# The order of sums over rows, gate products and slot matrices in a mixture-of-experts stage

## What is computed

```python
def expert_block(args):
    xb, gb = args
    h = jax.nn.silu(jnp.einsum('td,edf->tef', xb, w_gate)) * jnp.einsum('td,edf->tef', xb, w_up)
    h = h * gb[..., None].astype(h.dtype)
    return jnp.einsum('tef,efd->td', h, w_down)
```

## Time and profile before

| | us |
|---|---|
| median of 3 runs | 1060.3 |
| lowest and highest | 1058.49, 1063.44 |
| the profiled execution | 1058.91 |
| its span, first to last instruction | 1056.7 |
| PE busy | 959.5 (91%) |
| VectorE busy | 530.8 (50%) |

### The profile page before, as it was taken

The page is one execution under the profiler, slowest core; times in us unless marked ns, Lnnn a source line. Parts: engine busy times, 40 slices in busy tenths (PEclk is TensorE's granted clock), DMA queues, the critical chain, the costliest instruction groups (busy, mean ns, idle before and its releaser), DMA issues.

```text
span 1056.7 us, 18183 instructions
## 1 busy us (share of the span) xinstructions
PE 959.5 (91%) x7418; PEld 567.7 (54%) x7418; DVE 530.8 (50%) x1061; ACT 234.4 (22%) x486; POOL 328.4 (31%) x362
## 2 busy tenths in 40 slices
PE   5999999999999987699998989979999999998995
PEld 4878877877787776448433334333333343333331
DVE  2148957875986678766133222121323223346665
ACT  3241134114312511433111111111111111111013
POOL 0049906961993499000111111010100110024310
PEclk9999999999999999899998889998999999999998
DMA  8635244525434247198799999999999999999951
GB/s 231 177 120 191 101 135 140 191 82 159 154 112 141 73 165 274 25 382 335 268 390 418 420 413 406 419 409 401 386 419 410 404 411 411 421 414 415 363 220 42
DMA packets 87358, 291.98 MB, mean 276 GB/s; under 512 B 17084, under 2 KB 48382, under 8 KB 62423
## 3 DMA queue, kind: packets, MB, share of 16 engines
q1 hardware_dynamic: 72647, 254.03, 62.7%
q0 software_dynamic: 14624, 36.74, 9.2%
HBM read 275.48 MB, written 32.63 MB: 292 GB/s over the span
## 4 chain that ended last, share of the span: by engine, by line
PE 66%; DMA 18%; DVE 8%; issue 3%; ACT 2%; SPq 2%; POOL 0%; DVEq 0%; POOLq 0%
PE bank L1358 63%; DMA big<-in_w_up 16%; PE bank L595 2%; ACT big L1655 2%; DMA big<-yrows,big 1%; DMA big<-in_w_in 1%; DVE big L1945 1%; SPq L400 1%; PE bank L626 1%; DVE big L1056 1%; DVE big L1998 1%; DVE big L990 1%; DVE big L2002 0%; ACT L1655 0%; DVE big L1153 0%
## 5 line engine op out<-in xcount | busy, mean ns | idle before, releaser
L1358 PE MATMUL bank<-big 64*64 64x64 f32 (+8 forms) x6930 | 894.8, 357 | 75.9 <-DMA big<-in_w_up 23.5
L1358 PEld LDWEIGHTS bank<-big 64*64 64x64 f32 (+5 forms) x6930 | 511.5, 148 | 411.1 <-issue 317.2
L1655 ACT ACTIVATE big<-bank 128x512 f32<-128x512 f32 (+7 forms) x286 | 123.4, 453 | 659.6 <-PE bank L1358 385.5
L1159 POOL DMA_INDIRECT big<-xg,big x32 | 32.9, 1029 | 413.5 <-PE bank L595 337.3
L2149 POOL TENSOR_SCALAR big<-big 128x256 f32<-128x256 f32 x120 | 132.2, 1102 | 1.7
L981 DVE TENSOR_TENSOR big<-big,bank 128x256 f32<-128x256 f32 x32 | 13.5, 421 | 193.3 <-ACT big L1655 193.3
L2161 POOL TENSOR_TENSOR big<-big 128x256 f32<-128x256 f32 x120 | 94.3, 786 | 0.3
L1945 DVE SCALAR_TENSOR_TENSOR big<-big 128x256 f32<-128x256 f32 x120 | 79.6, 663 | 4.1
L990 DVE COPY big<-bank 128x512 f32<-128x512 f32 x32 | 22.1, 690 | 89.9 <-PE bank L1358 89.9
L1655 ACT ACTIVATE big<-big 128x272 f32<-128x272 f32 (+9 forms) x108 | 49.8, 505 | 42.3 <-DVE big L1880 11.3
L1655 ACT ACTIVATE big<-bank,big 128x272 f32<-128x272 f32 (+2 forms) x53 | 23.8, 476 | 112.4 <-PE bank L1358 112.4
(11 more groups left out here) (164 smaller groups left out, 443.5 us busy)
## 6 DMA issues: line engine op xcount, KB each, us to landing
big<-in_w_gate SPq DMA_DIRECT2D x64, 1024.0 KB, 15.2
big<-in_w_up SPq DMA_DIRECT2D x64, 1024.0 KB, 20.1
big<-in_w_down SPq DMA_DIRECT2D x64, 1024.0 KB, 12.7
big<-in_w_in SPq DMA_DIRECT2D x29, 1024.0 KB, 5.4
yrows<-big POOLq DMA_DIRECT2D x32, 512.0 KB, 3.5
big<-in_w_out SPq DMA_DIRECT2D x2, 2048.0 KB, 15.9
big<-in_state_wkv SPq DMA_DIRECT2D x32, 64.0 KB, 2.3
out_wkv_s<-big SPq DMA_DIRECT2D x32, 64.0 KB, 4.0
```

The lines of the kernel that those rows point to most:

```text
L1159: pool.indirect_dma_start(out=x[0:n, :], out_offset=None, in_=xg, in_offset=bass.IndirectOffsetOnAxis(ap=idxu[0:n, col:col + 1], axis=0), ...
L1358: return nc.tensor.matmul(out_, lhsT=lhsT, rhs=rhs, start=start, stop=stop)
L1655: return nc.scalar.activation(out_, in_, f, **kw)
```

## The change

On PE, `combine(q - 2)` stands behind the gate half `gate_up(q, 0, 4)` instead of ahead of it, and in those iterations `index(q + 3)` goes with it, behind the sum. In the other iterations the order is the old one. `turn_gates` waits for the first of the five additions of pair q-2 (the one that reads bank 0, which it writes) instead of for all five. On VectorE `late_gates` is split: the gate matrix (`gate_hots`) stands at the head of the iteration, then the slot matrix, then the additions; the copy of the turned gate matrix (`gate_copy`) stays behind the row list.

```diff
--- before.py
+++ after.py
@@ -653,7 +653,7 @@
 
                 pe.wait_ge(S['og_ready'], nlate(q) + 1)
                 wait(pe, 'g_ready', nlate(q))
-                wait(pe, 'cb_sum', NC * nlate(q - 1))
+                wait(pe, 'cb_sum', NC * nlate(q - 2) + (1 if late(q - 2) else 0))
                 pe.wait_ge(S['idx_ready'], 2 * min(q + 4, NPAIR))
                 for t in range(3):
                     r = tile_rows(t)
@@ -683,9 +683,7 @@
                     note(ins, 'cb_mm')
 
             for q in range(NPAIR):
-                if late(q - 2):
-                    combine(q - 2)
-                if q + 3 < NPAIR:
+                if q + 3 < NPAIR and not late(q - 2):
                     index(q + 3)
                 if q == 4:
                     count = pe.value_load(cnti[0:1, 0:1])
@@ -694,6 +692,10 @@
                 if DOWN_AT <= q < DOWN_AT + NDOWN:
                     shared_down(q - DOWN_AT)
                 gate_up(q, 0, 4)
+                if late(q - 2):
+                    combine(q - 2)
+                    if q + 3 < NPAIR:
+                        index(q + 3)
                 if q:
                     turn_hidden(q - 1)
                 if late(q):
@@ -990,14 +992,18 @@
                 note(v.tensor_copy(ye[q % NYE][:, 512:1024], ps_y[1][:, :]), 'ye_dve')
 
             def pair(q):
+                if late(q):
+                    gate_hots(q)
+                if q + 4 < NPAIR and late(q - 2):
+                    onehot(q + 4)
                 if late(q - 2):
                     add_late(q - 2)
                 if q + 3 < NPAIR:
                     fetch_rows(q + 3)
-                if q + 4 < NPAIR:
+                if q + 4 < NPAIR and not late(q - 2):
                     onehot(q + 4)
                 if late(q):
-                    late_gates(q)
+                    gate_copy(q)
                 ks = list(range(sums_by(q), sums_by(q + 1)))
                 ahead = len(ks) if q == NPAIR - 1 else len(ks) // 2
                 add_early(q, ks[:ahead])
@@ -1012,7 +1018,7 @@
                 if q == DOWN_AT + NDOWN - 1:
                     shared_rows(NDOWN - 1)
 
-            def late_gates(q):
+            def gate_hots(q):
                 wait(dve, 'g_mm', nlate(q))
                 link(v.tensor_tensor(OHg, K['slot'][:, 0:SLOTS].unsqueeze(1).unsqueeze(1)
                                      .broadcast_to([128, 3, 2, SLOTS]),
@@ -1020,6 +1026,8 @@
                                      ALU.is_equal), chain)
                 note(v.tensor_tensor(OHg, OHg, gate[:, :, 2 * PAIR[q]:2 * PAIR[q] + 2].unsqueeze(3)
                                      .broadcast_to([128, 3, 2, SLOTS]), M), 'og_ready')
+
+            def gate_copy(q):
                 dve.wait_ge(S['g_mm'], nlate(q) + 1)
                 wait(dve, 'cb_mm', NC * (nlate(q) - 5))
                 note(v.tensor_copy(GT[nlate(q) % 6], ps_gt[:, 0:NT]), 'g_ready')
```

## The result

The changed kernel takes 1064.4 us (median of 15 runs, 1058.5 to 1070.6), the kernel before 1060.9 us (median of 15 beside it, 1058.5 to 1063.5): a ratio of 1.0033, with a 95% interval of 1.0017 to 1.0049. The change makes the kernel 3.5 us slower. The forecast was 1061.0 us in a range of 1057 to 1067.5, and "no change that can be told" (within 0.5%) as the likeliest case.

What follows compares the result with a forecast made beforehand. The prediction took the expert stage as bound by weights streaming without pause, with PE nearly as busy. 0.9 - 0.8 + 0.7 = +0.8 us on 1058.9 gave 1059.7; on the median 1060.3, 1061.0 us, range 1057 to 1067.5.

Steps and rivals of the forecast that it cites:

- The removed wait: At eleven places in the expert stage, PE's gate half no longer waits for VectorE's copy: 16.1 us in all.
- the lost cover: At those places the gate half asks for weights 6.1 us sooner; pair 23's iteration ends 3.6 us later.
- The wait for the row list: PE's gate transposes wait for VectorE's next index list: 0.15 us a time, ends 0 and 0.6 us.
- The margin: At odd iterations' ends, slowest DMA engines still hold 3.4 us of work, so batches issued that much later land no later.
- the share of 0.68: DMA share from 760 to 764 us, around the issue at 761.94: part of the engines had run dry.
- The clock at the first place: At pair 15, PE idles 3.7 us, its clock falls and the gate half takes 1.4 us more.
- -0.8: At pair 31, hidden transposes begin at 1024.4 against 1025.18, 0.8 us earlier.
- The fall of the clock at the end: At the last places PE's clock may fall again: half of one fall, +0.7 us, ends none and 2.8.
- +0.9: Pair 15 ends 4.3 us later, 0.9 us beyond the 3.4 us in hand, moving all later landings by +0.9 us.
- The first rival: From odd iterations' batches, late issues delay landings and the stream runs dry: +14 us, or half, 1067 us; chance 0.17.
- its own "against": The objection to the stream running dry at odd iterations' batches: a shorter backlog shortens that very landing; no size given.
- The second rival: At all eleven places weights land sooner and all 16.1 us of waits go: 1044 us; chance 0.05.

Runs made afterwards that it cites:

- SP's other order in the late part: Changed kernel, with SP issuing gate and up matrices earlier and ahead of the down matrices from pair 14 on: 1052.1 us, ratio 0.9937 against the kernel before.

## Why the prediction was right in its range and wrong in its mechanism

*The removed wait* and *the lost cover* held. The copies' waits went, waits for up matrices came, 3.85 us at pair 15 (3.7 forecast), 0.3 to 2.4 us at the others (1 to 2), and the ends of the iterations with a sum are pinned to a landing: from pair 23's start at 882.73, 8.6 us to the transposes at 891.33. The wait for the row list measured 0.22 us (0.15 taken). VectorE's order costs nothing, and is needed: without it the change costs 20 us; the forecast had 1.1 us a time for that, where the wait alone was 1.66. The forecast also misread a row: the one at 879.24 is the gate matrix's first step (line 1017), not the slot matrix, and the 2.39 us are VectorE's wait ahead of its copy. The gate matrix was ready at 880.4, 1.8 us ahead of PE's transposes at 882.2.

*"A batch issued up to 3.4 us later lands no later. I take the landings as fixed by the stream"*: this step failed. The margin was read from the landing of the last up matrix in flight. Pair 15's batch came 6.4 us later than before (4.3 forecast), 3.0 beyond that margin, into engines that had been almost idle (a share of 0.11): its first up matrix, the fourth in the batch, landed 769.67 + 13.4 - 768.31 = 14.8 us after the batch's first issue. But a batch inside the margin fared no better. The batch at 801.38 was issued with the engines at 0.99 and 3.1 us ahead of the last landing (804.4), so by the prediction's own sum 1.0 us inside the margin (804.4 - 801.4 - 2.1), and its first up matrix landed 15.1 us after the issue (816.5); in the four rounds behind it, with 2.6 to 3.5 us to the last landing, it took 14.5 to 14.8. Before, it took 16.7 to 18.6 us at the same place, with 5.4 to 8.1 us to the last landing. So in these rows a batch that comes later is served faster only down to 14 to 15 us (13.8 at the least, with PE's order alone); from there a later issue is a later landing. The row that could have warned was in the prediction, the share of 0.68 with 3.4 us supposedly in hand; I noted it and trusted the landing. From the landing at 783.1 to the next late issue it is 801.38 - 783.1 = 18.3 us (18.0 in the prediction), so the loop is 14.8 + 18.3 = 33.1 us, the round as measured. Before, a round took 32.3.

*The clock at the first place* was taken as +1.4 us; the run stretched by 11.61 - 8.68 = 2.9, since the clock stayed at half for the first 6 us of it. *"-0.8" at the end* was too small as well: the four last iterations wait 0.31 + 2.42 + 1.31 us and not at all at pair 31, against 1.7 + 3.5 + 1.6 + 1.7 before, and that gives back 4.4 us. The fall of the clock at the end, taken as +0.7, changed next to nothing: before, it stood at 978.24 (9.61 us), now at 987.38 (9.73). So the profiled execution's account is: +6.2 at the end of pair 15 (768.31 - 743.44 = 24.9 against 18.7), +4 to +4.5 in five rounds of 0.8 to 0.9 us, some -4.3 at the end: +6.3. The forecast had +0.9 for the first, nothing for the rounds, and -0.8 and +0.7 for the end. Up to pair 25 the kernel had lost 10.8 us, more than the range allows; that the time stayed inside it is owed to the end, which was not foreseen at that size. In that the range held by luck.

*The first rival* had the mechanism and the place, and a price of +2.4 us a round at most, half of that as its middle; it was 0.8 to 0.9, since the landings came 14.5 to 15.1 us after the issue and not 16.7, as its own "against" had it. The end, which pays back 4 us, wasn't in its sum. *The second rival* (all 16 us) would need weights that don't bind; with SP's other order in the late part the changed kernel goes some of the way, -6.5 us between the two kernels with that order. The rule of the Trainium skill that the prediction weighed ("DMA: Bandwidth & Descriptors", rules for kernel authors: issue early, compute, wait late) agrees with the sign here: +3.5 us. By the last runs it is the late issue, the rule's first half, that costs: with the issue made earlier the same late compute gains.

## What to carry to other kernels

Work that stands ahead of a wait for a transfer is cover as long as the transfer lands inside it; before moving it behind the wait, add up the loop (issue to landing of the transfer needed first, plus landing to the next issue) and compare it with the round that the kernel has. Don't read a queue's reserve from the landing of its last transfer. A low share of busy engines just before the next issue tells that there is none, but here a share of 0.99 didn't tell that there was enough. What tells is how the time from issue to landing changes as the issue moves. And where that loop binds, look at what the issuing engine waits for and at the order in its queue first: a few lines on SP were worth more than the reordering on PE, and made the reordering pay.

## What was not expected of the hardware

A longer wait did not always bring the clock down where a shorter one did. PE waited 3.46 us ahead of 994.55 in the changed kernel with SP's late order, and its next run took the ordinary 8.03 us; in the changed kernel 2.42 us ahead of 987.38 were followed by 9.73. The granted clock of the two stretches (columns as above), the changed kernel first:

```profile
987.38:991.00 3.62, 3.62 (x12) 1.40 (x14) 2.65 (x4) 0.00 (x0) 2.40 (x3) 0.68 1.12 402
```

```profile
994.55:998.00 3.45, 3.45 (x16) 1.23 (x16) 0.00 (x0) 0.00 (x0) 0.00 (x0) 1.00 1.03 416
```

In the kernel with PE's order alone even 1.66 us were followed by a gate half of 5.35; there the wait stood between two groups of transposes. The length of the wait doesn't tell which. That may be part of why the changed kernel's runs spread over 12.1 us and those of before over 5.1; this was not tried.
